# Last attention pass of a one-core transformer block: eight output products start two steps sooner, three of the next eight move forward

## The reference

```python
def mla_mixer(h_lat, h_ctx, ...):
    ...
    o = lax.map(lambda q: attend(q[0], q[1], k_nope, k_rope, v), ...)   # 8 heads, 1280 keys
    o = jnp.moveaxis(o, 0, 1).reshape(b, n, N_HEADS * V_HEAD)
    y_lat = o @ w_o                                                      # the output product

def reference(...):
    ...
    x = x + g1 * y                                                       # gate and residual
    x = x + g2 * swiglu(modulate(rmsnorm(x, norm_ffn[i]), sh2, sc2), ...)
```

## Time and profile before

| | us |
|---|---|
| median of 3 runs | 2346.22 |
| lowest, highest of them | 2345.14, 2346.92 |
| the profiled execution, its own time | 2346.42 |
| its span in the profile | 2345.1 |
| PE busy in the span | 2319.5 (99%) |
| DVE, ACT, POOL busy | 1705.8, 807.3, 152.3 |

### The profile page before, as it was taken

How to read it: one execution, slowest core, us unless ns; L and a number is a source line. 1 busy time by engine, 2 the same in 40 slices (tenths; PEclk the granted TensorE clock), 3 DMA queues, 4 the chain that set the end, 5 groups by cost and what they waited for, 6 DMA issues and landing times.

```text
span 2345.1 us, 29300 instructions
## 1 busy us (share of the span) xinstructions
PE 2319.5 (99%) x11037; PEld 1919.1 (82%) x11037; DVE 1705.8 (73%) x2568; ACT 807.3 (34%) x1300; POOL 152.3 (6%) x114
## 2 busy tenths in 40 slices
PE   8999999999999999999999999999999999999998
PEld 5888888888888888888888888888888888888887
DVE  5778788886688888888886764264897777777776
ACT  6345545463443222222223511111532222222224
POOL 0121221100300000000001200000200000000002
PEclk9999999999999999999999999999999999999999
DMA  7001111123112333333332020120111111111112
GB/s 298 34 25 47 48 48 46 43 73 126 64 36 72 108 108 108 105 103 107 108 99 90 19 72 28 45 72 28 45 45 54 46 47 53 54 49 51 54 44 83
DMA packets 49208, 163.35 MB, mean 70 GB/s; under 512 B 5312, under 2 KB 8768, under 8 KB 48960
## 3 DMA queue, kind: packets, MB, share of 16 engines
q1 hardware_dynamic: 49088, 161.72, 20.6%
HBM read 157.51 MB, written 4.19 MB: 69 GB/s over the span
## 4 chain that ended last, share of the span: by engine, by line
PE 94%; DVE 3%; ACT 1%; POOL 1%; issue 0%; DMA 0%; SPq 0%; DVEq 0%; POOLq 0%; ACTq 0%
PE ps L628 26%; PE ps L630 26%; PE ps L629 26%; PE ps L1106 3%; PE ps L1040 2%; PE ps L1044 1%; PE ps L1042 1%; PE ps L1041 1%; PE ps L1045 1%; PE ps L1085 1%; PE ps L1087 1%; PE ps L1086 1%; PE ps L876 1%; PE ps L885 0%; PE ps L894 0%
## 5 line engine op out<-in xcount | busy, mean ns | idle before, releaser
L2212 DVE SCALAR_TENSOR_TENSOR x<-ps,mods,x 128x512 f32<-128x512 f32 x440 | 322.8, 748 | 147.0 <-PE ps L630 127.4
L628 PE MATMUL ps<-g_hi,w_hi 128*128 128x512 f32 (+1 forms) x848 | 328.2, 387 | 0.8 <-DVE x L2212 0.7
L630 PE MATMUL ps<-g_hi,w_lo 128*128 128x512 f32 (+1 forms) x848 | 327.1, 386 | 0.0
L629 PE MATMUL ps<-g_lo,w_hi 128*128 128x512 f32 (+1 forms) x848 | 327.0, 386 | 0.0
L628 PE MATMUL ps<-h_hi,op_hi 128*128 128x512 f32 x640 | 249.4, 390 | 0.0
L630 PE MATMUL ps<-h_hi,op_lo 128*128 128x512 f32 x640 | 249.2, 389 | 0.0
L1746 ACT CAST op_hi<-rq 128x512 fp32r<-128x512 f32 x240 | 146.6, 621 | 235.1 <-PE ps L630 229.8
L1757 ACT ACTIVATE g_full<-g_full 128x512 f32<-128x512 f32 x80 | 50.6, 633 | 491.0 <-DVE g_full L2564 491.0
L628 PE MATMUL ps<-h_hi,w_hi 128*128 128x512 f32 x512 | 200.5, 392 | 1.5 <-DVE ab L2462 1.4
L629 PE MATMUL ps<-h_lo,w_hi 128*128 128x512 f32 x512 | 199.4, 389 | 0.0
L630 PE MATMUL ps<-h_hi,w_lo 128*128 128x512 f32 x512 | 199.4, 389 | 0.0
(11 more groups left out here) (364 smaller groups left out, 4571.3 us busy)
## 6 DMA issues: line engine op xcount, KB each, us to landing
rq<-stream SPq DMA_DIRECT2D x80, 512.0 KB, 3.5
mod_raw_f<-ada_rows SPq DMA_DIRECT2D x48, 512.0 KB, 3.5
raw<-stream SPq DMA_DIRECT2D x46, 512.0 KB, 4.1
w_lo_f<-stream SPq DMA_DIRECT2D x46, 512.0 KB, 4.5
mod_raw<-ada_rows SPq DMA_DIRECT2D x32, 512.0 KB, 3.5
ada_ring<-ada_pe SPq DMA_DIRECT2D x16, 512.0 KB, 11.6
x<-x_t SPq DMA_DIRECT2D x8, 512.0 KB, 7.1
hraw<-head_w SPq DMA_DIRECT2D x8, 384.0 KB, 3.0
```

What stands on the lines that cost most here:

```text
L628: nc.tensor.matmul(out, w[0][wi], a[0][ai], start=start, stop=False)
L629: nc.tensor.matmul(out, w[0][wi], a[1][ai], start=False, stop=False)
L630: return nc.tensor.matmul(out, w[1][wi], a[0][ai], start=False, stop=stop)
L2212: nc.vector.scalar_tensor_tensor(out=x[:, m, HALF[half]], in0=ps[:, out_bank(d, m), :], scalar=mods[:, gate + m:gate + m + 1], in1=x[:, m, ...
```

## The change

The order of PE in the last pass is given by a table. Chunk (0, 0) stands at (gb 2, step 8), (0, 1) at (2, 9), the others of d 0 at steps 1 to 6 of group 3, and the first three chunks of d 1 at steps 7 to 9 of group 3. What is left behind the groups is (1, 3) to (1, 7), with `value_up` behind (1, 4). On DVE each `to_x(0, m)` comes one step sooner, and `mods_ready` (two small instructions that complete the gate vectors) two steps sooner.

```diff
+OUT_AT = {(2, 8): (0, 0), (2, 9): (0, 1), **{(3, m - 1): (0, m) for m in range(2, KD)},
+          (3, 7): (1, 0), (3, 8): (1, 1), (3, 9): (1, 2)}
@@
             elif kind == "PV":
-                if last_pass and gb == 3 and k >= 1 and k <= KD:
-                    out_part(D_OUT, k - 1)
+                if last_pass and (gb, k) in OUT_AT:
+                    d, m = OUT_AT[gb, k]
+                    out_part(D_OUT + d, m)
@@
-        for m in range(KD):
+        for m in range(3, KD):
             out_part(D_OUT + 1, m)
-            if m == 1:
+            if m == 4:
                 value_up(1, True)
@@
-                    if last_pass and gb == 3 and 2 <= k:
-                        to_x(D_OUT, k - 2, GATES[0])
-                    if last_pass and (gb, k) == (3, 1):
+                    if last_pass and gb == 3 and 1 <= k <= KD:
+                        to_x(D_OUT, k - 1, GATES[0])
+                    if last_pass and (gb, k) == (2, 9):
                         mods_ready()
```

## The result

The changed kernel takes 2350.4 us, median of 21 runs (2348.74 to 2353.46); the kernel before 2346.42 us, median of 21 (2344.76 to 2350.13). The ratio is 1.0018, 95% interval 1.0012 to 1.0023: 4.0 us slower by the medians, about as far as the 0.2% that tells a change from none. The profiled execution took 2348.89 us.

A forecast was written before the change was run, and what follows sets the result against it. PE was taken as the bound, busy 2319.5 of 2345.1 us. Terms 0.4 + 1.6 + 1.4 = +3.4, checked as +3.3 at `out_part(2, 0)`, on 2346.2 gave 2349.5 us, range 2346.6 to 2351.4.

The forecast's parts named there:

- The case named as likeliest: First rival, the sum as it stands: two tail waits and a front wait, +2.3 to +4.4 us; chance 0.64.
- Term one: End of group 2: the first chunk waits 2.1 us for the low part of `wo` 3; net +0.4 us.
- The 0.37 read as a wait for `olat`: Between `PV`(2, 9) and `PV`(3, 0): 0.37 us of waiting that the change does not touch.
- the 2.0 named as the most that can be won: End of group 2: at most 2.0 us of PE waiting could be removed.
- Group 3: Steps of group 3: one chunk each as before, 1.7 us to spare at the tightest; term 0.
- Term two: Behind `PV`(3, 9): chunk (1, 4) waits for `to_x(1, 0)` to free its bank; +1.5 us and 0.1 restart.
- Term three: At `out_part(2, 0)`: PE waits for the low part of `wo` 7; +1.3 us and 0.1 restart.
- the rival of the late tile: Loads of `wo` 6 and 7 overlap and land late, PE waits longer: +2.5 more, +5.8 us in all; chance 0.08.
- the rival with 0.06: Slow clock after one of the three waits: 1.6 us more, +4.9 in all, 2351.1 us; chance 0.06.
- rows 10: Profile rows near the start: behind tiny matmuls the clock fell once to 0.50, then 0.68 in the next window.
- Within 0.2%, 0.84: Whole kernel: chance 0.84 that the time stays the same within 0.2%, which is 4.7 us.
- the chance for slower, 0.14: Whole kernel: chance 0.14 of being slower by more than 0.2%, from the late-tile and slow-clock cases.

The follow-up runs named there:

- c1: Changed kernel with the wait for the low part of `wo` 3 moved inside the first chunk and `value_up` behind (1, 3); 2346.76 us.
- c2: Changed kernel with two chunks of d 1 in group 3, `value_up` behind (1, 3), and the `wo` 3 wait inside the first chunk; 2344.05 us.
- b1: Changed kernel with `to_x(1, 0)` and `to_x(1, 1)` at (3, 9), `value_up` behind (1, 3), and the `wo` 3 wait inside the first chunk; 2344.62 us.
- a1: Changed kernel with `to_x(1, 0)` and `to_x(1, 1)` sooner on DVE, at (3, 9) ahead of `olat`; 2349.0 us.
- b2: Changed kernel with the front alone: d 0 starts at (2, 8), no chunk of d 1 inside group 3; 2348.53 us.
- a3: Changed kernel with only the wait for the low part of `wo` 3 moved inside the first chunk, ahead of the fourth head; 2350.52 us.
- b3: Changed kernel with `to_x(1, 0)` and `to_x(1, 1)` at (3, 9) and `value_up` behind (1, 3), front wait left; 2347.31 us.
- b4: Changed kernel with two chunks of d 1 in group 3 instead of three and `value_up` behind (1, 3); 2347.4 us.
- a0: The changed kernel run once more without edits, as base on its chip; 2350.43 us.
- a2: Changed kernel with `value_up` one chunk sooner, behind (1, 3) instead of (1, 4); 2347.61 us.
- c3: Repeat of b1 on another chip, all three edits to the changed kernel; 2345.01 us.
- d1: Repeat of c2 on another chip; 2343.86 us.

## Why the prediction was right, point by point

**The total.** Forecast 2349.5, range 2346.6 to 2351.4; measured 2350.4. The case named as likeliest, two tail waits and a front wait (+2.3 to +4.4), is what happened. At `out_part(2, 0)` +3.3 was worked out; the stretch grew by 3.67. The 0.4 between them are one term 0.5 too small and one 0.1 too large.

**Term one** (+0.4): the chunk starts 2.45 us after `T`(2, 9), and 2.46 was worked out; the wait reads 1.85 and not 2.1 because the profile counts it from the end of the rows of `T` (0.60), the working from its step of 0.35. From `T`(2, 9) to `PV`(3, 0) are 10.85 us, before 5.12: 5.73 more for 5.44 of chunks, so +0.3. The 0.37 read as a wait for `olat` was none: the profile shows no idle time there, before or after; `PV`(2, 9) behind a restart took 0.80 and the eight transposes 0.95 (532.62, 533.42, 534.37). The sum uses only the whole distance of 1.75, but the 2.0 named as the most that can be won came out as 1.8. What c1 adds is that this term, small as a sum, hides a large wait: with the wait inside, `T`(2, 9) to `PV`(3, 0) takes 8.76 us (528.34 to 537.10), 1.8 less than 5.12 and the 5.44 of chunks. The kernel before lost that much there, in its waits for `pt_lo` and what they cost beside, and that is what c2 and b1 win.

**Group 3** (0): busy for 34.00 of 34.00 us. Right.

**Term two** (+1.5, 0.1 restart): the last product of chunk (1, 3) starts at 577.65, the next would follow 0.22 later, at 577.87, and PE went on at 579.36: 1.49. `to_x(1, 0)` began at 578.55 and ended at 579.29. a1 shows by taking it away that it is worth 1.5. Right in place, cause and size.

**Term three** (+1.3, 0.1 restart): PE, free at 591.05 (579.36 + 2.85 + 0.68 + 8.16), went on at 592.85: 1.8 where the working has 1.26, so this is the term that was undersized, by 0.5. The link that was off is the load of `wo` 7. From the end of `wo` 5's low part to ACT's cast of `wo` 7 are 4.32 us (586.12 to 590.44), taken as 3.51 from the earlier trace rows; for `wo` 6 it was 3.61 against 3.73. Of these 0.8 only 0.5 reached PE, because the working had DVE come to this low part 0.3 after ACT was through. The second load is issued 1.8 us behind the first, where it was 3.4 before. This is the small end of the rival of the late tile: its mechanism was there, its 2.5 us were not. The loads of `wo` 6 and 7 from issue to landing, first in b2, where they are issued 3.4 us apart as before, then in the changed kernel:

```profile
DMA to landing us min/median/max: 3.4/3.5/3.5
...
DMA to landing us min/median/max: 3.5/3.9/4.3
```

With only two loads the first and the last figure are the two of them. In the two profiles with 3.4 us between the issues (before and b2) both took 3.4 to 3.6; in all twelve with 1.8 between them the first took 3.3 to 3.9 and the second 4.3 to 4.9. So the longer second load goes with the shorter distance between the issues in all fourteen, whatever else was edited. That they share the DMA engines is the likely reason, and it is argued.

**The clock.** Half right. The sum took no loss, and in the two profiled executions of the changed kernel there was none. But the rival with 0.06 was under-rated. It happened in four of the eight profiled executions that hold a wait of 1.8 us or more (a3, b2, b3, b4; not in the changed kernel, a0, a1, a2), in none of the six others (before, b1, c1, c2, c3, d1), and cost 1.6 to 1.8 us each time. The reason given against it, "PE before and behind it is dense, unlike in rows 10", does not hold. Nor does "once": the trace of before has a second fall in its last 20 us, at 2330, again behind tiny matmuls (0.96, 0.50 and 0.68 in the windows from 2328 to 2334), and a third from 2340 on (0.50 in the window from 2342). Such falls may be why the medians differ by 4.0 and 4.9 where the stretch differs by 3.7; the unprofiled runs show only a mean clock over the whole kernel, so that stays argued.

**Within 0.2%, 0.84.** The measured 0.18% is within, at the edge, and the second group of runs (a0) gave 0.21%: the chance for slower, 0.14, looks too low.

## What to carry to other kernels

Work moved to where an engine idles only pays if its own inputs are there: find the last input that it needs, and put the wait at the instruction that uses it, not at the start of the block. Here three of four heads could run ahead of the fourth tile, and that turned a wait of 1.9 us into nothing.

Work moved forward is cover taken from behind: the third chunk moved was the cover of `to_x(1, 0)` and of the last weight tile, and two chunks gave all that three could. Count what stood between a producer and its user before the move, and what stands there after.

Judge by a stretch between two instructions that bound the change, then look at the clock behind its end: waits inside it and clock lost behind it must both be counted before a null result is called "no gain".

## What the runs showed of the hardware

Four times in eight a wait of about 1.9 us of PE in the middle of dense products of 128x512, with PE busy throughout for microseconds on both sides, was followed by a fall of the granted clock to the level of 1.2 GHz. It began 0.5 to 1.5 us after PE had gone on, and the loss was 1.6 to 1.8 us each time. It fell in some executions and not in others with the same instructions and the same wait (b3 and the changed kernel). A wait of this size thus costs 1.9 us in one execution and 3.6 in another. Shorter waits inside the stretch, up to 1.75 us (`wo` 7 in a1), were not followed by a fall in these profiles. What decides it is open, and the chip is not ruled out: the three falls behind the front wait (b2, b3, b4) are all on the chip of group b, the four front waits without one (changed, a0, a1, a2) on others. Against the chip alone speaks that the quickest of the eleven runs of b4 is 1.85 us over the quickest of b1 on that same chip (2344.82 and 2342.97), which is the wait without a loss of clock; but that compares two lowest values.

The Trainium skill (TensorE: Matmul & The Clock Gate, section "HAM oscillation — how this bites in real kernels") describes this pattern, waits between groups of matmuls after which the next group starts cold; the trace agrees on the pattern, and the price of 1.6 to 1.8 us is this case's own. The same page of the Trainium skill (section "What's actually happening") says that how many products run at the lower level at a kernel's start differs from run to run of one kernel; b3 against the changed kernel shows such a difference in the middle, 1.7 us against none.

Apart from these four falls, the clock fell in two other places of the fourteen profiled executions: in six of them between 24 and 32 us, and in all of them in the last 20 us. The first place moves the time of an execution that holds no wait of this change. c2 and d1 are one program with stretches of 58.96 and 58.94 us, and their profiled executions took 2345.31 and 2343.44 us; c2 had the fall near the start and reached `T`(2, 9) 1.19 us later. The window there in c2, then in d1:

```profile
24.00:32.00 8.00, 6.82 (x32) 5.71 (x32) 5.91 (x18) 6.29 (x16) 0.00 (x0) 0.79 1.05 384
...
24.00:32.00 8.00, 6.92 (x38) 5.86 (x38) 6.09 (x18) 6.48 (x16) 0.00 (x0) 1.00 1.05 385
```

So the spread of eleven runs does not tell the versions apart. c2 and d1, with no wait in the stretch, span 2.4 and 2.2 us, but so do a0 and a3, with waits of 1.9 (2.4 and 2.2); b4, with one such wait, spans 5.2, but b1 and c3, with none, 5.3 and 4.8. The slower executions of b1 and c3 were not profiled, so what happened in them stays open.
